# Latent attention on one core: keys projected with features on partitions, only queries transposed

## What is computed

```python
q    = (rms_norm(h @ w_dq) @ w_uq).reshape(512, 16, 64 + 32)
kv_a = h @ w_dkv                                  # 256 latent columns and 32 rotary ones
c_kv, k_rope = rms_norm(kv_a[:, :256]), rotate(kv_a[:, 256:])     # one k_rope for all heads
kv   = (c_kv @ w_ukv).reshape(512, 16, 64 + 64)   # per head: 64 key columns, 64 value columns
logits = (q_nope @ k_nope.T + rotate(q_rope) @ k_rope.T) * 96 ** -0.5     # causal
out  = softmax(logits) @ v                        # then @ w_o
```

## Time and profile before

| | us |
|---|---|
| median of 3 runs (1860.54 to 1863.26) | 1860.9 |
| the profiled execution, own time | 1860.39 |
| its span in the trace | 1858.3 |

### The profile page before, as it was taken

The page is one execution under the profiler, slowest core; times in us unless marked ns, Lnnn a source line. Parts: engine busy times, 40 slices in busy tenths (PEclk is TensorE's granted clock), DMA queues, the critical chain, the costliest instruction groups (busy, mean ns, idle before and its releaser), DMA issues.

```text
span 1858.3 us, 22186 instructions
## 1 busy us (share of the span) xinstructions
PE 1804.3 (97%) x8737; PEld 1437.9 (77%) x8737; DVE 875.9 (47%) x1321; ACT 752.2 (40%) x1248; POOL 635.6 (34%) x239
## 2 busy tenths in 40 slices
PE   7999999999998999999999999999999999999998
PEld 4887777777787767866988888888866798888886
DVE  6511466565837257954442222245367253333334
ACT  3324555546235253354432222227556352222322
POOL 1433122233224323422444433434400344433342
PEclk9999999999999999999999999999999999999999
DMA  7533212222131312311232233222300222233222
GB/s 284 204 96 111 88 58 70 57 68 65 49 114 53 125 57 76 106 46 57 70 113 91 90 100 103 90 91 77 107 7 1 91 91 91 91 100 103 90 91 80
DMA packets 83377, 165.08 MB, mean 89 GB/s; under 512 B 5977, under 2 KB 8158, under 8 KB 83294
## 3 DMA queue, kind: packets, MB, share of 16 engines
q1 hardware_dynamic: 83294, 163.95, 26.9%
HBM read 157.64 MB, written 2.10 MB: 86 GB/s over the span
## 4 chain that ended last, share of the span: by engine, by line
PE 72%; issue 16%; DVE 5%; POOL 4%; ACT 2%; DMA 1%; SPq 0%; POOLq 0%; DVEq 0%; ACTq 0%
PE PDT L656 12%; PE PDT L658 11%; PE PDT L657 11%; PE PDT L667 7%; PE PDT L669 7%; PE PDT L668 7%; POOL wlo L1897 4%; PE PM L1220 1%; PE PDT L1220 1%; PE PM L1259 1%; PE PM L1199 1%; PE PM L704 1%; PE PDT L797 1%; PE PDT L802 1%; PE PDT L796 1%
## 5 line engine op out<-in xcount | busy, mean ns | idle before, releaser
L1897 POOL TENSOR_TENSOR wlo<-wraw,whi 128x2048 fp32r<-128x2048 f32 (+4 forms) x166 | 612.1, 3696 | 1048.5 <-ACT whi L1375 1009.5
L1375 ACT ACTIVATE whi<-wraw 128x2048 fp32r<-128x2048 f32 (+2 forms) x133 | 247.8, 1863 | 537.9 <-PE PDT L658 318.9
L667 PE MATMUL PDT<-hhi,whi 128*128 128x512 f32 x800 | 314.8, 393 | 0.8 <-POOL wlo L1897 0.8
L669 PE MATMUL PDT<-hhi,wlo 128*128 128x512 f32 x800 | 311.7, 390 | 0.0
L668 PE MATMUL PDT<-hlo,whi 128*128 128x512 f32 x800 | 311.5, 389 | 0.0
L656 PE MATMUL PDT<-whi,hhi 128*128 128x512 f32 (+1 forms) x612 | 242.2, 396 | 0.7 <-POOL wlo L1897 0.7
L657 PE MATMUL PDT<-wlo,hhi 128*128 128x512 f32 (+1 forms) x612 | 235.8, 385 | 0.0
L658 PE MATMUL PDT<-whi,hlo 128*128 128x512 f32 (+1 forms) x612 | 235.8, 385 | 0.0
L656 PE MATMUL PDT<-whi,mh_hi 128*128 128x512 f32 x512 | 202.5, 396 | 0.0
L658 PE MATMUL PDT<-whi,mh_lo 128*128 128x512 f32 x512 | 202.5, 396 | 0.0
L657 PE MATMUL PDT<-wlo,mh_hi 128*128 128x512 f32 x512 | 202.4, 395 | 0.0
(11 more groups left out here) (344 smaller groups left out, 2418.7 us busy)
## 6 DMA issues: line engine op xcount, KB each, us to landing
wraw<-in_mlp_w SPq DMA_DIRECT2D x64, 1024.0 KB, 5.2
wraw<-in_w_in SPq DMA_DIRECT2D x26, 1024.0 KB, 5.1
wraw<-in_even_w_in SPq DMA_DIRECT2D x16, 1024.0 KB, 5.3
w_ada<-in_w_ada SPq DMA_DIRECT2D x12, 1024.0 KB, 13.7
wraw<-in_w_out SPq DMA_DIRECT2D x8, 1024.0 KB, 5.1
swapped<-qk_sb SPq DMA_DIRECT2D x16, 256.0 KB, 6.7
wraw<-in_even_w_out SPq DMA_DIRECT2D x4, 1024.0 KB, 5.0
wraw<-in_odd_w_o SPq DMA_DIRECT2D x4, 1024.0 KB, 5.2
```

The costliest lines, as they stand in the source:

```text
L667: mm(bank, sth, hi[:, k0 + k, :], start=start and k == 0, stop=False)
L669: last = mm(bank, stl, hi[:, k0 + k, :], start=False, stop=stop and k == 3)
L1375: nc.scalar.activation(whi[base % 2][:, 0:n], wraw[base % 2][:, 0:n], ACT.Copy).then_inc(S("w_hi"), 1)
L1897: part = g.tensor_tensor(wlo[base % 2][:, cols], wraw[base % 2][:, cols], fl(whi[base % 2][:, cols]), ALU.subtract)
```

## The change

The keys are computed with features on partitions, so that they need no transposition, and stay in one buffer `kt3` (96 partitions, 16 heads, 512 positions).

- Each of the two `ukv` units is rearranged while ACT rounds it and POOL splits it: the key columns of its eight heads first, the value columns behind (`parted`, `halves`). For these units both engines do two instructions of 1024 columns instead of one of 2048.
- PE makes, per unit, four key banks (weights as the stationary operand: 128 features, two heads, by 512 positions) and four value banks (positions on partitions). ACT empties a key bank with two instructions of 64 partitions x 512, one for each head, and a value bank with one of 128 x 512.
- DVE rotates the shared 32 columns before it waits for `uq`; PE transposes them once, behind the first unit's products (`turn_k_rope`, 4 transpositions); ACT copies the result into rows 64 to 95 of head 0 of `kt3`; SP then spreads these rows to heads 1 to 3, 4 to 9 and 10 to 15 by three DMAs, which stand in its queue behind the load of the first `wo3` unit and ahead of the load of the second. PE waits for each of the three before the first head that needs it.
- The queries of head 0 are turned within the last value products, into `PM`; those of head 1 after them, into `PDT`. In the head loop only the queries are turned. `kth`, `k_tm`, `turned_k` and the copy of the rotary columns to 16 heads are gone.
- ACT rounds the first `wo3` unit after it has copied the queries of head 1, no longer before the second half of `ukv`. POOL's split of that unit follows it.
- Buffers move: `v3`, `pr3`, `prt3`, `mx3`, `den3`.

The diff, with unchanged lines left out:

```diff
@@ -97,7 +97,7 @@
...
-            ("cq", 3, 1), ("ckv", 2, 1), ("heads", 2 * C_H + C_H // 2, 0), ("ffn1", 8, 1)]
+            ("cq", 3, 1), ("ckv", 2, 1), ("heads", 1 + C_H + C_H // 2, 0), ("ffn1", 8, 1)]
@@ -260,17 +260,17 @@
...
-    k_tm = arena("k_tm", [P, TT, C_H, C_QK], 51)
-    v3 = arena("v3", [P, TT, DM], 75)
+    kt3 = arena("kt3", [C_QK, C_H, SEQ], 51)
+    v3 = arena("v3", [P, TT, DM], 83)
...
-    kth = [arena(f"kth{s}", [P, SEQ], 4 + 2 * s) for s in range(2)]
-    pr3 = [arena("pr30", [P, 1280], 8), arena("pr31", [P, 1280], 16)]
-    prt3 = [arena(f"prt3{s}", [P, 1280], kb) for s, kb in enumerate((21, 91, 96))]
-    prt3.append(at("prt33", [P, 1280], offset=place["row_a"]))
+    pr3 = [arena("pr30", [P, 1280], 9), arena("pr31", [P, 1280], 16)]
+    unused_half = place[f"whi{(PH['wo3'][0] + 1) % 2}"]
+    prt3 = [arena("prt30", [P, 1280], 4), arena("prt31", [P, 1280], 21), at("prt32", [P, 1280], offset=unused_half),
+            at("prt33", [P, 1280], offset=place["row_a"])]
...
-    mx3 = arena("mx3", [P, 4, TT], 13)
-    den3 = arena("den3", [P, 4, TT], 13.5)
+    mx3 = arena("mx3", [P, 4, TT], 26)
+    den3 = arena("den3", [P, 4, TT], 26.5)
@@ -318,6 +318,17 @@
...
+    KEYS_VALUES = [PH["ukv"][0] + n for n in range(2)]
+    K_SPREAD = [(1, 4), (4, 10), (10, C_H)]
+    def parted(w, unit, k):
+        return w[unit % 2][:, 1024 * k:1024 * k + 1024].rearrange("p (h c d) -> p c h d", c=2, d=HD)
+    def halves(w, unit, k):
+        return w[unit % 2][:, 1024 * k:1024 * k + 1024].rearrange("p (c h d) -> p c h d", c=2, d=HD)
@@ -410,16 +421,16 @@
...
-    def head_group(h, m):
-        return TR["heads"][0] + 2 * h + m + max(0, (h - 4) // 2)
+    def head_group(h):
+        return TR["heads"][0] + 1 + h + max(0, (h - 4) // 2)
...
-        return TR["heads"][0] + 2 * min(C_H, 2 * pair + 6) + pair
+        return TR["heads"][0] + 1 + min(C_H, 2 * pair + 6) + pair
@@ -619,7 +630,15 @@
         u0 = PH["ukv"][0]
         for n in range(2):
...
-        columns("wo3", w_oo_v, 2, 0)
+        u0 = PH["wo3"][0]
+        for n in range(4):
+            h = n % 2
+            if n == 1:
+                sp.wait_ge(S("tr_read"), TR["heads"][0] + 1)
+                for m, (first, end) in enumerate(K_SPREAD):
+                    load(kt3[C_NOPE:C_QK, first:end, :],
+                         kt3[C_NOPE:C_QK, 0:1, :].to_broadcast([C_QK - C_NOPE, end - first, SEQ]), f"k_rope_spread{m}")
+            unit(u0 + n, (u0 + h) % 2, 4, 512, w_oo_v[:, 4 * h:4 * h + 4, 512 * (n // 2):512 * (n // 2) + 512])
@@ -1306,44 +1325,66 @@
...
+        def turn_k_rope():
+            pe.wait_ge(S("mla_roped"), 1)
+            for t in range(TT):
+                last = nc.tensor.transpose(PM[0:C_QK - C_NOPE, 2, t * P:t * P + P], kva[:, t, 256:288], ident[:, :])
+            last.then_inc(S("tr_done"), 1)
+        def turn_q(h):
+            if h == 0:
+                pe.wait_ge(S("mla_roped"), 2)
+            elif h >= 2:
+                pe.wait_ge(S("tr_read"), head_group(h))
+            X = PDT if h else PM
+            for t in range(TT):
+                last = nc.tensor.transpose(X[0:C_QK, 3, t * P:t * P + P], q_tm[:, t, h * C_QK:h * C_QK + C_QK], ident[:, :])
+            last.then_inc(S("tr_done"), 1)
+        def key_product(ws, b):
+            wh, wl = wview(whi[ws], 2, 1024), wview(wlo[ws], 2, 1024)
+            for k in range(2):
+                sth, stl = [w[:, k, P * b:P * b + P] for w in (wh, wl)]
+                mm(PD[b], sth, hhi[:, 3 + k, :], start=k == 0, stop=False)
+                mm(PD[b], sth, hlo[:, 3 + k, :], start=False, stop=False)
+                last = mm(PD[b], stl, hhi[:, 3 + k, :], start=False, stop=k == 1)
+            return last
+        def value_product(ws, t):
+            return tm(PD[t], 512, (hhi, hlo), 3, ws, 2, 1024, 512, True, True, t)
         u0 = PH["ukv"][0]
         for n in range(2):
             unit_wait(u0 + n)
-            for r in range(2):
-                for t in range(TT):
-                    bank_wait("ukv", t, 2 * n + r)
-                    last = tm(PD[t], 512, (hhi, hlo), 3, (u0 + n) % 2, 2, 1024, 512 * r, True, True, t)
-                    if t == 3 and r == 0:
-                        last.then_inc(S("bank_full3"), 1)
-                    else:
-                        full(last, t)
-        pe.wait_ge(S("mla_roped"), 1)
+            for b in range(4):
+                bank_wait("ukv", b, 2 * n)
+                key_product((u0 + n) % 2, b).then_inc(S(f"bank_full{b}"), 1)
+            for t in range(TT):
+                bank_wait("ukv", t, 2 * n + 1)
+                if (n, t) == (1, 3):
+                    turn_q(0)
+                full(value_product((u0 + n) % 2, t), t)
+            if n == 0:
+                turn_k_rope()
         phase_done(pe, "ukv")
-        def turn_qk(h, m):
-            pe.wait_ge(S("tr_read"), head_group(h, m))
-            for t in range(TT):
-                src = k_tm[:, t, h, :] if m else q_tm[:, t, h * C_QK:h * C_QK + C_QK]
-                last = nc.tensor.transpose(PDT[0:C_QK, 3, t * P:t * P + P], src, ident[:, :])
-            last.then_inc(S("tr_done"), 1)
-        for h in range(2):
-            turn_qk(h, 0)
-            turn_qk(h, 1)
+        turn_q(1)
         for h in range(C_H + 3):
...
                 probs_taken(n - 1)
-                pe.wait_ge(S("tr_read"), head_group(h, 1) + 1)
-                qh, kh = qth[h % 2], kth[h % 2]
-                logits(n, lambda t: qh[0:C_QK, t * P:t * P + P], lambda w: kh[0:C_QK, 0:w])
+                pe.wait_ge(S("tr_read"), head_group(h) + 1)
+                for m, (first, end) in enumerate(K_SPREAD):
+                    if h == first:
+                        pe.wait_ge(S(f"k_rope_spread{m}"), 16)
+                logits(n, lambda t: qth[h % 2][0:C_QK, t * P:t * P + P], lambda w: kt3[:, h, 0:w])
...
-                turn_qk(h + 2, 0)
+                turn_q(h + 2)
             if 1 <= h <= C_H:
                 turn_probs(n - 1, pr3)
-            if h + 2 < C_H:
-                turn_qk(h + 2, 1)
@@ -1372,6 +1413,10 @@
...
+            if isinstance(i, int) and base in KEYS_VALUES:
+                nc.scalar.activation(halves(whi, base, 0), parted(wraw, base, 0), ACT.Copy)
+                nc.scalar.activation(halves(whi, base, 1), parted(wraw, base, 1), ACT.Copy).then_inc(S("w_hi"), 1)
+                return
@@ -1835,28 +1880,34 @@
...
+        def turned_q(h):
+            act.wait_ge(S("tr_done"), head_group(h) + 1)
+            X = PDT if h else PM
+            nc.scalar.activation(qth[h % 2][0:C_QK, :], X[0:C_QK, 3, :], ACT.Copy, scale=-C_QK ** -0.5)\
+                .then_inc(S("tr_read"), 1)
         u0 = PH["ukv"][0]
+        hi(0, u0 + 1, 0)
         for n in range(2):
-            hi(0, u0 + n + 1, 0)
-            for r in range(2):
-                for t in range(TT):
-                    if t == 3 and r == 0:
-                        act.wait_ge(S("bank_full3"), PH["ukv"][2][3] + n + 1)
-                    else:
-                        full_wait(act, "ukv", t, 2 * n + r, u0 + n)
-                    h0 = 8 * n + 4 * r
-                    kv = PD[t].rearrange("p (h d) -> p h d", h=4)
-                    nc.scalar.activation(k_tm[:, t, h0:h0 + 4, 0:C_NOPE], kv[:, :, 0:64], ACT.Copy)
-                    nc.scalar.activation(v3[:, t, h0 * HD:(h0 + 4) * HD].rearrange("p (h d) -> p h d", d=HD),
-                                         kv[:, :, 64:128], ACT.Copy).then_inc(S(f"bank_free{t}"), 1)
-        def turned_q(h):
-            act.wait_ge(S("tr_done"), head_group(h, 0) + 1)
-            nc.scalar.activation(qth[h % 2][0:C_QK, :], PDT[0:C_QK, 3, :], ACT.Copy, scale=-C_QK ** -0.5)\
-                .then_inc(S("tr_read"), 1)
-        turned_q(0)
+            for b in range(4):
+                if b == 3:
+                    act.wait_ge(S("bank_full3"), PH["ukv"][2][3] + n + 1)
+                else:
+                    full_wait(act, "ukv", b, 2 * n, u0 + n)
+                h0 = 8 * n + 2 * b
+                nc.scalar.activation(kt3[0:C_NOPE, h0, :], PD[b][0:HD, :], ACT.Copy)
+                nc.scalar.activation(kt3[0:C_NOPE, h0 + 1, :], PD[b][HD:P, :], ACT.Copy).then_inc(S(f"bank_free{b}"), 1)
+            for t in range(TT):
+                if (n, t) == (1, 3):
+                    turned_q(0)
+                full_wait(act, "ukv", t, 2 * n + 1, u0 + n)
+                nc.scalar.activation(v3[:, t, 512 * n:512 * n + 512], PD[t], ACT.Copy).then_inc(S(f"bank_free{t}"), 1)
+            if n == 0:
+                act.wait_ge(S("tr_done"), TR["heads"][0] + 1)
+                nc.scalar.activation(kt3[C_NOPE:C_QK, 0, :], PM[0:C_QK - C_NOPE, 2, :], ACT.Copy)\
+                    .then_inc(S("tr_read"), 1)
...
+        hi(0, u0 + 2, 0)
...
         for h in range(C_H + 4):
@@ -1891,6 +1942,11 @@
...
+            if isinstance(i, int) and base in KEYS_VALUES:
+                for k in range(2):
```

(17 more changed lines are left out.)

## The result

| us | before | after |
|---|---|---|
| median | 1862.08 (1860.1 to 1864.49, 6 runs) | 1851.93 (1849.55 to 1857.23, 6 runs) |
| ratio, 95% interval | | 0.995 (0.9936 to 0.9964) |
| the profiled execution, own time | 1860.39 | 1850.24 |
| its span | 1858.3 | 1848.5 |

The change makes the kernel faster by some 10 us. The page of the profile says where to look: PE lost 1804.3 - 1796.0 = 8.3 us of work and the span 9.8, so 1.5 us of PE's gaps went as well.

A forecast was written before the change was run, and what follows sets the result against it. PE was taken to bound the kernel, with ACT as close in short rounds. -4.1 - 3.4 - 2.6 = -10.1 us (the +0.88 inside the 4.1) took 1860.39 to 1850.3; the median, 0.5 above, was 1850.8, range 1848 to 1856.

The forecast's parts named there:

- What bounds the kernel: Whole kernel: PE, busy 97% of the span; short head rounds bound by PE and ACT within 0.1 us, long ones by PE.
- The product stage, +0.88: `ukv` products: same 96 matmuls, plus transpositions of the rotary columns and head 0's queries, 2 x 0.44 = 0.88 us.
- The rearranged unit: Rounding and split of `ukv` units: still in time for PE, slack about 0.8 us at the first, 3.6 at the second.
- Rival B: POOL's rearranged split is late and PE waits: 1852.3 at 1.5 times today's time, 1854.1 at twice; chance 0.11.
- C: POOL's split: each 64-element run costs a set-up, making the kernel slower than before, 1864 at 15 us a unit; chance 0.05.
- The start, -4.1 net: Last product to first logits: three hand-overs through one bank gone, logits at 1348.5 instead of 1352.58, 4.1 us less.
- The first two rounds, -3.4: First to third logits: 7.7 us instead of 11.1, about 2.1 of the gain from first logits at full clock.
- rival A: Start of the heads: PE's clock falls all the same, costing 3 to 5 us, 1854 to 1856; chance 0.11.
- The rounding's cover: ACT's moved `wo3` rounding ends 0.1 us before its next job, queries 2; without that cover at most 1.9 us cost.
- The loop, -2.6: Head loop: key transpositions gone, long rounds 3 to 13 give 6 x 0.44 = 2.6 us, short rounds 2 to 12 give 0.
- The DMAs, 0: Three transfers of rotary rows land by 1344, 1356 and 1368, before their heads need them; cost 0.
- Rival D: No difference: the transfers are late and head 1 waits, 7.5 us of the gain gone, 1858; chance 0.07.

The follow-up runs named there:

- the two pads: `pad_short` and `pad_long`: the kernel after with four unused PE transpositions put back in six rounds of one kind; 1849.84 and 1855.51 us.
- rounding_back: Kernel after, with ACT's rounding of the first `wo3` unit put back ahead of the second half of `ukv`; 1850.98 us.
- one_spread: Kernel after, with one DMA of 960 KB in place of the three that spread the rotary rows; 1856.64 us in its one run.
- before_filled: Kernel before, with six unused transpositions behind each of the four turns of heads 0 and 1; 1862.79 us, ratio 1.0002.
- queries_shared: Kernel after, with the queries' copy moved from ACT to DVE in rounds 0 to 2 and the even ones alone; 1850.53 us.
- pad_short: Kernel after, with four unused PE transpositions in each of the even (short) rounds 2 to 12; 1849.84 us, ratio 0.9946.
- pad_long: Kernel after, with four unused PE transpositions in each of the odd (long) rounds 3 to 13; 1855.51 us, ratio 0.9971.
- queries_by_dve: Kernel after, with the queries' copy of heads 2 to 15 moved from ACT to DVE in all rounds; 1850.38 us, ratio 0.9953.
- before_four_banks: Kernel before, with each of the four start turns of queries and keys in a PSUM bank of its own; 1856.23 us, ratio 0.9979.

## Why the prediction was right, point by point

It gave 1850.8 with 1848 to 1856, and the median is 1851.93. Of the profiled executions it gave 1850.3, and 1850.24 was measured. The mechanism held, but that both numbers agree so closely is in part luck. The stretch gained 10.57 and not 10.1, and the profiled execution of the kernel after was 0.88 us later than that of before when the stretch began (1293.71 against 1292.83). The median depends on how many of the six executions were long ones (last section): the same kernel timed once more gave 1857.01, beyond the forecast's 1856, with the stretch unchanged.

- **What bounds the kernel.** Right, and the two pads show it: the same 2.6 us of work cost 2.65 in long rounds and 0.42 in short ones. The wait forecast for short rounds is there.
- **The product stage, +0.88.** Measured +0.95.
- **The rearranged unit.** Its split had a slack of 0.75 us where about 0.8 was forecast: it ended at 1319.71 + 4.75 = 1324.46, and ACT's last copy of `uq` was released at 1325.21. The two halves took 4.75 us for one unit, against 4.62 in one piece. POOL by time (start us, us, line, shapes, idle time before and its releaser):

```profile
1319.71 4.75 POOL L1947 TENSOR_TENSOR wlo<-wraw,whi 128x1024 fp32r<-128x1024 f32 x2 [4.86 <-ACT whi L1418]
1327.88 6.20 POOL L1947 TENSOR_TENSOR wlo<-wraw,whi 128x1024 fp32r<-128x1024 f32 x2 [3.41 <-ACT whi L1418]
```

  Runs of 64 elements thus cost 3%, not 50%: rivals B and C fall. The Trainium skill, page "GPSIMD Engine Reference", section on performance pitfalls, puts its surcharge on reads with a step of over 8 bytes, which these aren't, and this case's 4.75 us agree with that. (Rival B at twice today's time should have read 1850.8 + 3.8 = 1854.6 as a median, not 1854.1; nothing hangs on it.) The second split, beside DVE's rotation, took 6.20 instead of 5.07. It ended at 1334.08 and PE's first product of that unit began at 1336.25, 2.2 us later (forecast 3.6, before DVE got in between).
- **The start, -4.1 net.** Measured -4.2.
- **The first two rounds, -3.4.** Measured -3.34, with the clock at 1.00 all through, so rival A falls: one wait of 1.09 us on PE, ahead of the third logits, didn't bring the clock down here, nor in the three other profiles with this start (`after_again`, `rounding_back`, `one_spread`), whose stretches are 148.71 to 148.76. `before_filled` prices the lower clock at 2.1 us of these 3.3 by itself, as the forecast had it. The rounding's cover was 0.27 us (forecast 0.1); ACT by time:

```profile
1349.80 1.90 ACT L1420 ACTIVATE whi<-wraw 128x2048 fp32r<-128x2048 f32 x1
1351.97 0.59 ACT L1886 ACTIVATE qth<-PDT 96x512 f32<-96x512 f32 x1 [0.27 <-PE PDT L1343]
```

  POOL's split behind it, from 1351.78, had DVE's minima beside it, and the first of them took what such an instruction took ahead of the split, at 1350.17 (0.70):

```profile
1352.77 0.70 DVE L2514 CUSTOM_DVE_ANT_0 PDT<-PDT,causal 128x512 f32<-128x512 f32 x1 [0.48 <-PE PDT L1239]
```

- **The loop, -2.6.** This is the term that was mis-sized: -3.03. The step was "Short rounds 2 to 12: ACT sets the start of the next logits as before, so 0". ACT's bound was there, but 0.14 us below the old round and not at it. In the rows, ACT's copy ended at 1391.81 while PE's own work lasted to 1392.00, and after the change the logits start 0.04 us behind such a copy: the 0.19 between them, less this hand-over, is the 0.14 to 0.15. It was nearly all in the rows, and I took it for zero. Round by round, the five short rounds 4 to 12 give 5 x 0.14 = 0.7. Round 2, which has no values to multiply, was already held by ACT, with a wait of PE ahead of the next logits, and gives 0.03 (5.26 before, 5.23 after). The long rounds 5 to 13 give 5 x 0.37 = 1.85, not 5 x 0.44, since logits behind a wait now take 0.07 more; before round 3 there was such a wait already, so that it gives its full 0.43 (6.42 before, 5.99 after). Together 3.0, as measured: the short rounds brought more than forecast and the long ones less (2.3 instead of 2.6), and the two errors cancel in part.
- **The DMAs, 0.** SP issued them from 1337.3 on, and no instruction of PE waited for them. They landed ahead of the forecast's bounds of 1344, 1356 and 1368 (issues, KB each, median us to landing):

```profile
kt<-kt SPq DMA_DIRECT2D x2, 384.0 KB, 5.6
kt<-kt SPq DMA_DIRECT2D x1, 192.0 KB, 4.4
```

  Rival D falls, and `one_spread` shows how far away it was.

## What to carry to other kernels

Before pricing work that is taken out of a loop, ask for each kind of round which engine is late next and by how much; the difference to that engine is all there is to gain, and a pad of unused work put back into one kind of round at a time measures it. Hand-overs through a single PSUM bank at the start of the heads cost twice in the profiled execution, once as waits and once through the clock, and separate banks took away nearly half of what this whole change did. Moving work off the bounding engine pays only after the waits on its bank are followed as well: all rounds together gained nothing, the chosen ones 1.75 us.

## What the runs showed of the hardware that was not expected

**More than one level of time in one kernel.** The kernel after was profiled and timed once more, as it is, and the version with shared queries too, once as it is and once with unused transpositions of the identity (4, 8 and 8) in PE's three waits at the start of another attention, at about 820 us:

```diff
+            if h == 1:
+                fill(4)
             if 1 <= h <= A_H:
                 turn_probs(h - 1, pr)
+            if h in (1, 2):
+                fill(8)
```

> The kernel after, unchanged, on the same chip and in the same rounds as the run beside it, for a direct comparison: stretch 148.7 us, and a time 1.4 us above that run by the theory, equal to it by the rival.

> queries_shared unchanged, on the same chip beside the run with filler: by the theory some executions near 1848.5 and some near 1855.5; the stretch between the two splits 147.0 us in either.

> The kernel queries_shared, with filler transpositions in TensorE's three waits (0.7, 1.1 and 1.1 us) in rounds 1 and 2 of the other attention, at about 818 to 826 us, outside the change. Theory (the same kernel ran either near 1850 or near 1857 us, and in the trace of a long execution the granted clock stood at 0.50 from 821 to 835 where a short one had 1.00; the fall follows these waits): no execution near 1855 or above, all within 2 us of 1848.5, clock 1.00 in 820 to 840. Rival (the clock falls there whatever TensorE does, or filler of short transpositions isn't enough): both levels, 7 us apart, still appear.

`after_again`: 1857.52, 1857.35, 1849.13, 1850.15, 1849.26, 1857.78 and 1857.01 us, two groups 7 us apart; median 1857.01, ratio 0.9955 (0.9936 to 0.9973). The kernel beside it in the same rounds, `queries_shared`, has a median 6.5 us lower, where the stretch is 1.8 shorter: such medians don't tell these kernels apart. The stretch of `after_again` is 148.76, so the 7 us lie elsewhere. The busy times of 820 to 830 us, first of the profile after (1850.24 us), then of `after_again` (1857.52):

```profile
820.00:830.00 10.00, 7.75 (x40) 5.02 (x42) 7.12 (x22) 6.14 (x19) 1.17 (x2) 1.00 0.00 1
```

```profile
820.00:830.00 10.00, 8.15 (x20) 4.91 (x21) 4.37 (x13) 3.86 (x14) 1.18 (x2) 0.54 0.00 0
```

The granted clock was 1.00 in one and 0.54 in the other. PE by time, the same two kernels in the same order:

```profile
821.11 2.40 PE L1239 MATMUL PM<-qkt 64*128 64x512 f32 x8 [1.14 <-DVE prt L2521]
```

```profile
820.71 4.43 PE L1239 MATMUL PM<-qkt 64*128 64x512 f32 x8 [1.14 <-DVE prt L2521]
```

The wait ahead is 1.14 us in both, and the logits take 2.40 at one level and 4.43 at the other (1.2 GHz). So the same waits bring the clock down in some executions and leave it up in others. All 13 profiles can be read for this, by the granted clock (a mean over 10 us of what stood at one level or the other) and by the time from the start of POOL's split at about 800 us to that of its next one:

| profiled executions | clock, 820 to 830 us | split to split, us |
|---|---|---|
| `before` (1860.39), after (1850.24), `pad_short`, `pad_long`, `queries_by_dve`, `queries_shared`, `shared_again`, `shared_and_filled` | 1.00 | 60.4 |
| `rounding_back` (1853.43), `before_four_banks` (1859.17) | 0.67 | 65.2 |
| `after_again` (1857.52), `one_spread` (1856.64), `before_filled` (1865.12) | 0.50 to 0.54 | 68.0 |

The longest and the shortest differ by 7.6 us, all that separates `after_again` from the first profile of its kernel, and there is a level between them. The Trainium skill, page "TensorE: Matmul & The Clock Gate", part 1, says of the start of a kernel that the number of matmuls at the lower clock differs from execution to execution, because what the chip looks at is not tied to the kernel's start, and it puts that penalty under 1% of a typical kernel's span. Here the same is seen in the middle of a kernel, and 7 us of 1850 are 0.4%.

This place doesn't explain all. `pad_long` reached 1860.94, 10.6 above its profiled execution, so that something else costs 3 us in some executions. And the kernel before, at 1860.39 with the short 60.4, would stand at 1868.0 with 68.0, while none of the 31 executions of it beside the pads is over 1865.98. Perhaps its start doesn't bring the clock down each time; then the 2.1 and 3.0 us that the clock cost there hold for the profiled execution and not for all, which would also fit that `before_filled` shows no gain in its median. No second profile of the kernel before was taken, so this stays open.

With the fillers the five executions were 1847.1, 1847.37, 1845.77, 1847.04 and 1847.73 (ratio 0.9922, 0.9908 to 0.9935), and 820 to 840 us ran at 1.00; the same kernel without them took 1846.11 to 1854.51 (median 1849.79; 0.9942, 0.9926 to 0.9957). The stretch is 146.94 and 146.96. The fillers don't shorten the shorter executions (split to split is 60.4 with and without them); in these five the longer ones don't occur. Five are few: that the longer ones are gone is likely, not shown. This is the fastest version, 14 us under the kernel before by the medians of the same rounds.

**A DVE instruction with two operands in SBUF seems to wait for POOL's whole instruction.** Before, one rotation step took 5.63 us instead of 1.23 beside POOL's split. After, with the split in two instructions, two steps took 3.41 each (DVE by time):

```profile
1327.27 1.22 DVE L2100 TENSOR_TENSOR rtm<-q_tm,sinm 128x1024 f32<-128x1024 f32 x1
1328.41 3.41 DVE L2100 TENSOR_TENSOR rtm<-q_tm,cosm 128x1024 f32<-128x1024 f32 x1
1331.75 3.41 DVE L2100 TENSOR_TENSOR rtm<-q_tm,sinm 128x1024 f32<-128x1024 f32 x1
```

POOL's first half ended when its second began, at 1330.7, and the first slow step ended at 1328.41 + 3.41 = 1331.82, 1.1 us later. The second half ended at 1334.08 and the second slow step at 1335.16, again 1.1 later. Before, the split ended at 1326.90 + 5.07 = 1331.97 and the step at 1327.43 + 5.63 = 1333.06, once more 1.1 later. Each time that is about as long as such a step takes by itself (1.22). A much smaller step was caught as well, the last of the shared rotary columns, beside a split of 128x1536; the two of them together took 0.36 us before, where POOL was idle:

```profile
1311.27 3.66 DVE L2100 TENSOR_TENSOR kva<-rtm 128x64 f32<-128x64 f32 x2
1311.29 3.56 POOL L1953 TENSOR_TENSOR wlo<-wraw,whi 128x1536 fp32r<-128x1536 f32 x1 [5.04 <-ACT whi L1420]
```

I read it as one POOL instruction awaited by each such step, so that two pieces can make DVE wait twice. A run that changes only the size of POOL's pieces was not made. POOL paid too: its second unit took 6.20 us. It cost PE nothing here: the rotated queries were not needed until 1346.
